# Splitting the last block's second stage into two halves of 64 tokens, and issuing the end's weight tiles as places come free

## The reference

```python
z = einsum('bhqd,bhkd->bhqk', qb, kb)                 # stick-breaking attention, per block of 128 queries
log_keep = where(before, log_sigmoid(-z), 0.0)
log_stick = cumsum(log_keep, axis=3, reverse=True) - log_keep
w = where(before, exp(log_sigmoid(z) + log_stick), 0.0)
mask = (pos[None, :] // 64) <= (pos[:, None] // 64)   # spatial gating: rows 0-63 of a chunk read rows 0-63 only
merged = sigmoid(g_a) * (y_a @ w_up_a) + sigmoid(g_b) * (y_b @ w_up_b)
x = x + merged @ w_out
```

## Time and profile before

| | us |
|---|---|
| median of 3 runs | 1957.14 (1956.62 to 1957.34) |
| the profiled execution's own time | 1955.42 |
| its span | 1953.6 |
| PE busy | 1634.3 (84%) |
| DVE busy | 1328.8 (68%) |
| ACT busy | 656.3 (34%) |
| POOL busy | 600.0 (31%) |
| HBM read | 725.63 MB, 373 GB/s over the span |

### The profile page before, as it was taken

One profiled execution on the slowest core, in us unless ns is written; L12 is line 12 of the kernel. 1 busy time (PEld: TensorE's weight loads), 2 busy tenths in 40 slices (PEclk: granted clock), 3 DMA queues, 4 the chain that ended last, 5 costly groups with the idle time before them and its releaser, 6 DMA issues.

```text
span 1953.6 us, 19684 instructions
## 1 busy us (share of the span) xinstructions
PE 1634.3 (84%) x6534; PEld 799.7 (41%) x6534; DVE 1328.8 (68%) x3466; ACT 656.3 (34%) x1224; POOL 600.0 (31%) x529
## 2 busy tenths in 40 slices
PE   7987897779889976888589999789986877877998
PEld 7555553235455443244145434333333322322453
DVE  4356877875788797875876577976665569744242
ACT  3222424242343254222231233521221246311472
POOL 1002333432333343334433333343323325422000
PEclk9997998889999998889899999899998988899999
DMA  7559999999999998999999999999999999999863
GB/s 223 179 169 416 417 417 419 408 417 418 386 413 354 355 416 326 380 419 415 422 413 418 418 414 374 362 400 418 419 417 350 418 419 401 421 418 412 326 235 109
DMA packets 128836, 729.03 MB, mean 373 GB/s; under 512 B 14688, under 2 KB 15856, under 8 KB 63200
## 3 DMA queue, kind: packets, MB, share of 16 engines
q0 software_dynamic: 74272, 537.82, 67.5%
q1 hardware_dynamic: 54464, 189.97, 25.5%
HBM read 725.63 MB, written 2.10 MB: 373 GB/s over the span
## 4 chain that ended last, share of the span: by engine, by line
PE 47%; DMA 23%; DVE 18%; ACT 5%; issue 5%; POOL 1%; POOLq 0%; DVEq 0%; SPq 0%; ACTq 0%
PE pa L919 26%; DMA uv_rows<-in_peer_uv,small 14%; PE py L919 13%; DMA wbuf<-in_wt 8%; PE pb L919 7%; DVE uv_rows L2046 6%; ACT area L1371 2%; ACT L1365 2%; POOL uv_rows L2291 1%; DVE tk L2056 1%; DVE area L2144 1%; DVE tk L2055 1%; DVE small L2033 1%; ACT small L1371 1%; DVE small L1951 0%
## 5 line engine op out<-in xcount | busy, mean ns | idle before, releaser
L2291 POOL DMA_INDIRECT uv_rows<-in_peer_uv,small x512 | 592.2, 1157 | 1182.3 <-PE py L919 967.2
L2046 DVE CUSTOM_DVE_ANT_0 uv_rows<-uv_rows,xrep 128x1024 f32<-128x1024 f32 x512 | 615.7, 1223 | 223.5 <-DMA uv_rows<-in_peer_uv,small 220.6
L919 PE MATMUL py<-uv_rows,tk 128*64 128x512 f32 x2048 | 560.8, 674 | 211.8 <-DVE tk L2056 208.1
L919 PE MATMUL pa<-wbuf,area 128*128 128x512 f32 (+2 forms) x784 | 342.0, 587 | 27.4 <-DMA wbuf<-in_wt 26.7
L1371 ACT ACTIVATE small<-small 128x2 f32<-128x2 f32 (+4 forms) x327 | 70.6, 217 | 849.9 <-DVE small L2046 816.2
L919 PEld LDWEIGHTS py<-uv_rows,tk 128*64 128x64 f32 x2048 | 135.7, 148 | 514.6 <-DVE tk L2056 278.3
L1365 ACT ACT_TABLE_LOAD x250 | 320.8, 1283 | 5.4 <-DVE small L2177 1.0
L919 PE MATMUL pa<-area,wbuf 128*128 128x256 f32 (+2 forms) x1280 | 233.7, 341 | 17.5 <-issue 12.0
L919 PEld LDWEIGHTS pa<-area,wbuf 128*128 128x128 f32 x1280 | 201.3, 199 | 70.6 <-issue 44.5
L919 PEld LDWEIGHTS pa<-wbuf,area 128*128 128x128 f32 (+1 forms) x784 | 134.2, 189 | 229.5 <-issue 176.5
L1371 ACT ACTIVATE area<-pa 128x512 f32<-128x512 f32 (+7 forms) x225 | 89.2, 413 | 267.3 <-PE pa L919 238.0
(11 more groups left out here) (253 smaller groups left out, 1178.0 us busy)
## 6 DMA issues: line engine op xcount, KB each, us to landing
wbuf<-in_wt SPq DMA_DIRECT2D x300, 512.0 KB
uv_rows<-in_wt SPq DMA_DIRECT2D x36, 512.0 KB, 6.6
uv_rows<-in_peer_uv,small POOLq DMA_INDIRECT x512
wbuf<-in_skT SPq DMA_DIRECT2D x11, 256.0 KB
h<-in_x SPq DMA_DIRECT2D x4, 512.0 KB
an<-in_x SPq DMA_DIRECT2D x3, 512.0 KB
out<-h SPq DMA_DIRECT2D x3, 512.0 KB, 8.3
area<-in_finw SPq DMA_DIRECT2D x2, 512.0 KB, 10.1
```

The lines of the kernel that those rows point to most:

```text
L919: return nc.tensor.matmul(o, l, r, start=start, stop=stop, skip_group_check=True)
L2046: last = V.tensor_tensor_reduce(uv_rows[:, n % RING, 0:D], uv_rows[:, n % RING, 0:D], xrep[:, b % 2, n % TG, :], 1.0, 0.0, ALU.mult, ALU.a ...
L2291: nc.gpsimd.indirect_dma_start(uv_rows[:, n % RING, :], None, t["peer_uv"], bass.IndirectOffsetOnAxis(ap=expert_ids[:, c:c + 1].bitcast(U3 ...
```

## The change

The last block's 128 tokens become two halves of 64 with names of their own, `HALVES = (4, 5)`: 4 is tokens 0 to 63 of block 3, 5 is tokens 64 to 127.

- The gathers of block 3 are put in another order: the first 64 (ticks 192 to 223) are for half 4, the other 64 (ticks 224 to 255) for half 5 (`gather_column`, `tokens_of`). Half 4 then has its first stage complete after tick 223. Since every head is needed by tick 220, the searches get denser: from tick 142 on one head for every 6 ticks, not 8 (`chosen_part`).
- `POST` is now (0, 1), (2, 4), (5,). The group (2, 4) has a plan of its own, `late_rows`, over the same last 49 ticks. Block 2's `q2`, `k2`, `v2` and attention come first, half 4's `q2r`, `k2r`, `v2` (12 tiles of its own) from tick 225 on, and all other tiles serve both, two per tick, in ticks 231 to 255 (without 251).
- A half has a layout of its own: 64 tokens by 512 columns are kept as 128 partitions by 256 columns, with columns 256 to 511 in partitions 64 to 127. `product` therefore issues two matmuls of 256 columns with 64 stationary columns each, into the lower and the upper partitions of one bank, where a block has one of 512 columns. Attention of a half takes two heads in one unit (four units, where block 3 had eight).
- The end is `last_rows` for half 5 alone: the same 60 tiles. Its plan is shorter by four units; `fin`, `fd` and `store` of block 2 and of half 4 stand in it.
- Sums over a row that lies in two halves of the partitions need a `fold` (three small DVE instructions). Stores of a half take two DMAs for one.
- The end's first tile no longer waits for the last gather (`if n == TAIL` goes).

```diff
-POST = [(0, 1), (2,), (3,)]
+HALVES = (NB, NB + 1)
+POST = [(0, 1), (2, HALVES[0]), (HALVES[1],)]
...
+LATE = 49
+FIRST_HALF = 17
+
+def late_rows(g):
+    b, h = g
+    rows = [[] for _ in range(LATE)]
...
+    at = {(b, u): 6 + 2 * u for u in range(n_units(b))}
+    at.update({(h, u): FIRST_HALF + 7 + 2 * u for u in range(n_units(h))})
...
+    put(FIRST_HALF, ("ldhalf",), ("hu", h))
...
+    for i, pair in enumerate(pairs_of(tiles("q2", (b,)) + tiles("k2", (b,)) + tiles("v2", (b,)))):
+        put(i, *pair)
+    own = tiles("q2r", (h,)) + tiles("k2r", (h,)) + tiles("v2", (h,))
+    both = [s for name in ("vb", "ub", "zb", "za") for s in tiles(name, g)]
+    for gate, up in (("gb", "ud"), ("ga", "ua")):
+        for c in range(2):
+            both += tiles(gate, g, c) + [(up, g, c, i) for i in range(2)]
+    for i, pair in enumerate(pairs_of(own + both)):
+        put(t + i, *pair)
+    for i, pair in enumerate(pairs_of(tiles("wo", g, 0) + tiles("wo", g, 1))):
+        put(t + 27 + i, *pair)
...
 def last_rows(b):
...
-    between = {0: ("hx", b), 2: ("ln", b), 3: ("l2", b), 4: ("sg", b), 5: ("yb", b)}
+    between = {0: ("hx", b), 1: ("ln", b), 2: ("l2", b), 3: ("sg", b), 4: ("yb", b)}
+    k, h = POST[1]
+    more = {3: [("fin", k)], 4: [("fd", k), ("store", k), ("fin", h)], 5: [("fd", h), ("store", h)]}
...
+DENSE = PER_HEAD * 17 + 6
+
+def chosen_part(k):
+    if k < DENSE:
+        return k // PER_HEAD + LEAD, k % PER_HEAD
+    return 17 + LEAD + 1 + (k - DENSE) // 6, (k - DENSE) % 6
...
+        def gather_column(n):
+            if n < GATHERS - SLOTS:
+                return n % (2 * SLOTS)
+            n -= GATHERS - SLOTS
+            return SLOTS * ((NB - 1) % 2) + TOP * (n % (SLOTS // 2) // PER_HEAD) + TG * (n % PER_HEAD) + n // (SLOTS // 2)
...
                 elif SPOTS[n] >= NW:
                     sp.wait_ge(uv_free, GATHERS - RING + 2 * BATCH)
-                if n == TAIL:
-                    sp.wait_ge(uv_full[RING - 1], 16 * (GATHERS // RING))
...
+            def product(ps, b, rows_, w, start, stop):
+                if b not in HALVES:
+                    return mm(ps[:, :], rows_, w, start, stop)
+                for q in range(2):
+                    last = mm(ps[side(q), 0:H], rows_, w[:, H * q:H * (q + 1)], start, stop)
+                return last
...
                 for j, ps in enumerate(open_banks):
                     for k in range(2):
-                        last = mm(ps[:, :], src[:, k0 + 2 * i + k, P * j:P * (j + 1)], w[:, k, :],
-                                  i + k == 0, i == n_tiles - 1 and k == 1)
+                        last = product(ps, g[j], src[:, k0 + 2 * i + k, P * j:P * j + rows_of(g[j])], w[:, k, :],
+                                       i + k == 0, i == n_tiles - 1 and k == 1)
...
+                if b == NB - 1:
+                    m, final = HALVES[k // (PER_BLOCK // 2) % 2], (k + 1) % (PER_BLOCK // 2) == 0
+                    for i in range(BATCH):
+                        n = BATCH * k + i
+                        for c in range(2):
+                            last = mm(psum_y[c][cell(m, c), :], mix_w[k % 2][:, i, :], uv_rows[:, n % RING, D + W * c:D + W * (c + 1)],
+                                      False, final and i == BATCH - 1)
+                    last.then_inc(uv_free, BATCH)
+                    return
...
                 ps = b_bank()
+                if b in HALVES:
+                    for part in range(2):
+                        mm(ps[side(part), 0:nk], q[side(part), u, :], k2T[side(part), u, 0:nk], True, False)
...
+            def fold(dst, src, ready):
+                step(V.tensor_copy(half_sw[side(0), 0, 0:src.shape[1]], src[side(1), :]))
+                step(V.tensor_copy(half_sw[side(1), 0, 0:src.shape[1]], src[side(0), :]))
+                last = V.tensor_tensor(dst, src, half_sw[:, 0, 0:src.shape[1]], ALU.add)
```

More of the change, by code:

```diff
@@ L76, in units2 @@
 def units2(g):
-    return [(b, u) for b in g for u in range(H2 // heads_per_unit(b))]
+    return [(b, u) for b in g for u in range(n_units(b))]
 def tiles(name, g, *more):
@@ L235, in second_rows @@
     for c in range(2):
[L236 to L243, removed]
+        rows += pairs_of(tiles("ga", g, c), 1) + [[("ua", g, c, i) for i in range(2)]]
+        rows += pairs_of(tiles("gb", g, c), 1) + [[("ud", g, c, i) for i in range(2)]]
     b = g[-1] + 1
     rows += [[("mt", k) for k in g] + [("ldnorm",)]]
-    wo = shared(wo, 6)
+    wo = shared(tiles("wo", g, 0) + tiles("wo", g, 1), 6)
     for i, name in enumerate(("n1", "m1", "n2")):
@@ L268, in last_rows @@
             row.append(between[n])
-        if n < n_units:
-            row += [("zp", b, n // 2)] * (n % 2 == 0) + [("zl", b, n)]
-        rows.append(row + fill[n])
+        if n < n_units(b):
+            row.append(("zs", b, n))
+        rows.append(row + more.get(n, []) + [s for k in fill[2 * n:2 * n + 2] for s in k])
     rows += [[("ya", b)], [("yo", b)]] + [[("ua", g, c, i) for i in range(2)] for c in range(2)]
@@ L413, in make_plan @@
     ticks[at + 5].append(("ldfinal",))
-    spread(second_rows((2,)), 3 * PER_BLOCK + 15, n, ticks)
+    for k, row in enumerate(late_rows(POST[1])):
+        ticks[n - LATE + k] += row
     place_keys(ticks)
@@ L770, in is_last, with half_index, own_rows, cell @@
             return g == POST[-1]
+        def half_index(b):
+            return b - HALVES[0]
+        def own_rows(b):
+            return slice(TOK * half_index(b), TOK * (half_index(b) + 1))
+        def cell(b, c):
+            at = c if b == HALVES[0] else 1 - c
+            return slice(TOK * at, TOK * (at + 1))
+        def side(q):
+            return slice(TOK * q, TOK * (q + 1))
+        def turned(g):
+            all_ = POST_OF[g[0]]
+            if is_last(all_):
+                return hT_last
+            at = sum(rows_of(b) for b in all_[:all_.index(g[0])])
+            return cut(hT_words[:, 0:KT * width(all_)], KT, width(all_))[:, :, at:at + width(g)]
@@ L1593, in _, with take_quarter_columns @@
+            def take_quarter_columns(dst, ps, end=True):
+                for i in range(2):
+                    last = fn(dst[:, i::2, :], cut(ps[:, P * i:P * (i + 1)], 2, TOK), ACT.Copy)
+                if end:
+                    last.then_inc(a_free, 1)
+            weighed, turned_n = 0, 0
             for s in PLAN:
@@ new lines, in half_rows_up @@
+                    V.tensor_tensor(an[r, 0:W], psum_y[c][r, :], weights, ALU.mult).then_inc(u_ready, 1)
+                ps = cut(bank()[:, :], 4, P)
+                for c in range(2):
+                    last = V.tensor_tensor(turned((b,))[:, 4 * c:4 * c + 4, :], ps[:, :, cell(b, c)],
+                                           normg2[:, 4 * c:4 * c + 4].unsqueeze(2).broadcast_to([P, 4, TOK]), ALU.mult)
+                emptied(last)
+                dve.wait_ge(sq_done, m + 1)
+                fold(half_tot[:, m, :], half_ss[:, m, :], ss_ready)
@@ L2084, in last_products, with half_out @@
+            def half_out(b):
+                col = 16 + nth(b)
+                dve.wait_ge(rf_done, nth(b))
+                dve.wait_ge(ld_f, 16)
+                for q in range(2):
+                    last = V.scalar_tensor_tensor(x1(b)[side(q), :, :], x1(b)[side(q), :, :], rs[side(q), col:col + 1],
+                                                  cut(fw[side(q), :], 2, 2, H)[:, :, q, :], ALU.mult, ALU.mult)
+                last.then_inc(fin_ready, 1)
             def last_products(b, c):
-                half = slice(W * c, W * (c + 1))
+                col = 16 + nth(b)
```

718 lines of the change are left out of this document (438 added, 280 removed).

## The result

The median of the change is 1968.99 us (1964.43 to 1973.18) against 1957.85 for the kernel before on the same chip (1954.18 to 1966.72). The ratio is 1.0054, 95% interval 1.0044 to 1.0064: slower, by about 11 us. The forecast was 1944. The profiled execution has a span of 1968.1 us, against 1953.6.

A forecast was written before the change was run, and what follows sets the result against it. DMA was taken to bound the kernel until the last gather, PE the end. Ticks 1813.5 + 15.7 + 17 + 5 = 1851, plus end 89.5, gave 1940.5, 13 us less: 1957.1 - 13 = 1944 us, range 1918 to 1966.

The forecast's parts named there:

- Part 4: The end after the last tick's products: falls from 140.1 to 89.5 us, as a stream of tiles paced by DMA.
- Part 2: Ticks 231 to 255: PE becomes the bound, 203 us against DMA's 186, adding 17 us (0 to 45).
- The first sign named for a wrong forecast: The forecast is wrong if the ticks end beyond 1865.
- Part 1: Before the last gather: half 4's 12 own tiles and norm weights, 6.55 MB more, add 15.7 us.
- Part 3: Denser searches load DVE, chiefly in ticks 160 to 175: adds 5 us, bounds 0 and 12.
- Where the parts meet: End of the last tick's products, where ticks give way to the end: moves from 1813.5 to 1851.
- The hold at the stores: In the end, SyncE stands at block 2's and half 4's stores: end at T + 89.5, without it T + 80.
- T + 80: Finish of the end without the hold at the stores, counted from T = 1851, the last tick's products' end.
- The removed wait: End's first tile no longer waits for the last gather: counted as nothing; 0 to 4 us less if DMA stays bound.
- DMA as the bound to the last gather: Rival for the ticks: DMA stays the bound to the last gather, giving 1927 us; chance 0.22.
- the pairs in turn: Rival: a half's paired matmuls run one after another, 1.72 us a tile, giving 2035 us; chance 0.04.
- TensorE's order: Rival, ticks 231 to 244: PE's in-order waits for ACT or DVE eat the gain, 1979 at 2.5 us each; chance 0.17.

## Why the prediction was wrong

What bounds the ticks was foreseen, and the sizes lost the sign. The span of the forecast was 1940.5; it came out at 1968.1, 27.6 more. The step that failed most is Part 4, the end, 9.6 us too short; next is Part 2, TensorE's excess, some 6.5 too small; some 5.5 lie in ticks 207 to 255 beyond both, 1.9 in ticks 144 to 207, and 4.0 in the opening of that one execution. No one of these alone turns 13 us of gain into 11 of loss. The first sign named for a wrong forecast, ticks that end beyond 1865, came. By steps:

- **Part 1, more bytes (15.7).** Confirmed: with seven eighths of the own tiles gone, 13.2 us by their bytes, 14.0 went in the trace and 12 in the medians, all before tick 231. The page's HBM reads grew by 6.56 MB (725.63 to 732.19), as counted.
- **Part 2, TensorE in ticks 231 to 255 (17): right in kind, too small.** It was a difference, 203 - 186, and both terms erred the same way. TensorE took 204.9. In that, the changes of width were mis-sized: I took 0.1 from rows that gave 0.15 to 0.20, and 48 of them at 0.17 are 8.2 and not 4.8; the other prices together came out 1.5 too high. The transfers need 181.0 where I had 186: I charged them with all gathers and tiles of these ticks, 77.6 MB, and in the run without the half's products 74.0 MB move in them (409 GB/s over 181.0 us); the rest has landed when they begin. The excess is 23.9 (23.5 over ticks 207 to 255 as a whole), 6.9 more than forecast, 5.0 of it from the transfers' term. With a change at 0.17 alone it would have been near 20.
- The Trainium skill, "TensorEngine Tiling (Array Packing)", Tiling Modes (Key Properties), says that a change of tiling mode drains TensorE. The trace agrees that a change costs time: two changes less per tick made it 0.34 us shorter. The page gives no price; the run does.
- **Part 3, denser searches (5).** 4 us in the medians: right in size and wrong in place, so the size is luck. VectorE's bound ticks took the parts into their idle time and paid 0.9 us. The ticks that paid more are those with TensorE or DMA full (144 to 159 in the trace of before: TensorE 101.4 of 107.5 us, DMA 1.01; 176 to 206: DMA 1.00). Why they did was not tested.
- **Where the parts meet.** The last row products were forecast for 1851 and came at 1869.0. Of these 18 us, 4 are the opening of that one execution, and 1.9 lie in ticks 144 to 206, which took 6.9 more than before and not 5; the kernel before with denser searches has the same 7. Some 6.5 are Part 2's, and 5.5 lie in ticks 207 to 255 beside it: with the half's products left out these take 330.3 us, where the 309.1 of before and Part 1 make 324.8. About 3 of that is the stop at tick 224 by its DMA share (0.26 of 12 us), for which the forecast had nothing; the attempt to move it away won 2 at most. The rest, some 2.5 us, I can't assign.
- **Part 4, the end (89.5): 99.1, the step that failed most.** The hold at the stores was seen, and its price too: 9.5 forecast, 8.5 in the trace. What was wrong was the end without it, T + 80, which is 90.6. The stream of tiles ran as forecast, at DMA 1.02 to 1910 and 1.03 to 1930 with the stores last. But I let that stream set TensorE's end, 1 us behind the last tile, and gave TensorE's own waits nothing. With the stores last, the last tile lands at 1944.8 (1939.97 and 4.8 us), 76 us behind the last row products where I had 73, and TensorE ends at 1951.7, 6.9 us behind the tile. From 1914 on it waits for no tile; its end is the sum of 72.2 us of work (I had 71) and 11.0 of waits: 2.2 for tiles, and 8.8 for ScalarE and VectorE, of which 2.7 are behind the last attention unit and four are of 0.5 to 0.9 for transposed rows. The finish is a smaller part: from VectorE's last addition to the end 5.7 us were taken from the earlier trace rows, and it is 7.2 in the kernel after (1960.92 to 1968.1), with a fold between:

```profile
1960.92 0.41 DVE L2566 TENSOR_TENSOR h<-h,pb 128x256 f32<-128x256 f32 x1
```

- **The removed wait (0 to 4 us less).** Nothing, as taken.
- **Rivals.** DMA as the bound to the last gather is refuted by the windows, and the pairs in turn by the 0.875 us of a half's tile. TensorE's order (0.17, and the only slower one of weight) is not what happened either: 2.2 us of waits in 208. The slower outcome needed no waits, only a few tenths more on each tick: my own range of 1931 to 1957 for the sum left it no more than 13 us for terms that all came out longer.

Since a gain of 50 in the end was set against costs of 38 before it, each known to a tenth or two at best, 0.73 for faster was too sure.

## What to carry to other kernels

Moving work from a stretch that TensorE bounds into one that DMA bounds is free only until TensorE is full there: compute the room first (here 24 us idle in 115, against 41 us of products to go in), and count with it the attention and the changes of shape that come along; what lies beyond the room lengthens the stretch (here by 23.9 us). And where a stream of loads hides an engine's waits, add up that engine's work and waits by themselves too: in this end they came out longer than the stream. Where two groups share a stationary width change on every tile, order the products by width over two tiles. And look at what stands on the queue that issues the loads: a store whose rows are late holds every tile behind it, and putting it last gave 8 us here.

## What the runs showed of the hardware

- A change between 128 and 64 stationary columns costs TensorE 0.17 us (7.57 against 7.23 us per tick, two changes less, otherwise the same matmuls), as the mean of both directions.
- Two float32 matmuls of 64 stationary columns in the two halves of the array run side by side also for 256 columns: 32 of them in 3.50 us, 0.22 a pair, where one of 512 columns with 128 stationary columns has 0.43.
- After TensorE has stood 5.86 us in the end, its granted clock is 0.50, the lower level, and 16 matmuls take 3.68 us; at 1.00 the same 16 take 1.95.
- With DMA as the bound, a tile of 0.524 MB lands every 1.28 us (410 GB/s), and TensorE starts on the tiles of the end in exactly that step where nothing else comes between, as its timeline in the kernel after shows:

```profile
1898.85 1.08 PE L1114 MATMUL pa<-wbuf,area 128*64 128x256 f32 x8 [0.20 <-DMA wbuf<-in_wt]
1900.13 1.08 PE L1114 MATMUL pa<-wbuf,area 128*64 128x256 f32 x8 [0.20 <-DMA wbuf<-in_wt]
1901.41 1.08 PE L1114 MATMUL pa<-uv_rows,area 128*64 128x256 f32 x8 [0.19 <-DMA uv_rows<-in_wt]
```
